# Two-layer network on one core: the compression's products on parted operands, and the mixer's low parts of weights on VectorE

## What is computed

```python
for l in range(DEPTH):                                        # DEPTH = 2
    x = x + 0.5 * rms_norm(swiglu(rms_norm(x, g1), w_in1, w_out1), p1)
    x = x + rms_norm(token_mixer(rms_norm(x, g2), ...), p2)
    x = x + 0.5 * rms_norm(swiglu(rms_norm(x, g3), w_in2, w_out2), p3)

def compress(t, pos_emb, w1, b1, w2):        # t: 256 tokens, 2 groups, 64 features
    # 15 blocks of 32 tokens, stride 16, flattened to 2048 columns for each group
    flat = blocks_of(t) + pos_emb
    return gelu(flat @ w1 + b1) @ w2         # w1: 2048 x 256

def token_mixer(h, mem, ...):
    u, bg, cg, q, kv, nsa_g, q_mem, merge_g = split(h @ w_in)
    y_conv = bg * short_conv(cg * u, conv_w)
    k_cmp, v_cmp = compress(kv[0], ...), compress(kv[1], ...)
    y_nsa = nsa_attention(q, rope(q), k_cmp, v_cmp, rope(kv[2]), kv[3], rope(kv[4]), kv[5], gates)
    y_mem = attention(q_mem, mem)
    g_conv, g_nsa, g_mem = sigmoid(merge_g)
    return (g_conv * (y_conv @ w_conv) + g_nsa * (y_nsa @ w_nsa) + g_mem * (y_mem @ w_mem)) @ w_out
```

## Time and profile before

| | |
|---|---|
| time, median of 3 runs | 1868.53 us (1867.76 to 1871.23) |
| the profiled execution: time, span | 1868.0 us, 1866.1 us |
| mean granted TensorE clock | 0.982 |
| TensorE, weight loads | 1799.1 us (96%), 1590.8 us (85%) |
| VectorE | 1107.6 us (59%), 2045 instructions |
| ScalarE | 887.0 us (48%), 1403 instructions |
| GpSimd | 205.7 us (11%), 104 instructions |
| weights | 192 chunks of 1.5 MB, 311.68 MB moved in all, 167 GB/s |

### The profile page before, as it was taken

One profiled execution on the slowest core, in us unless ns is written; L12 is line 12 of the kernel. 1 busy time (PEld: TensorE's weight loads), 2 busy tenths in 40 slices (PEclk: granted clock), 3 DMA queues, 4 the chain that ended last, 5 costly groups with the idle time before them and its releaser, 6 DMA issues.

```text
span 1866.1 us, 30310 instructions
## 1 busy us (share of the span) xinstructions
PE 1799.1 (96%) x11888; PEld 1590.8 (85%) x11888; DVE 1107.6 (59%) x2045; ACT 887.0 (48%) x1403; POOL 205.7 (11%) x104
## 2 busy tenths in 40 slices
PE   6999999999899999999999999899999999999988
PEld 5999898888789989999798988799979988767876
DVE  6555474436665556555671458455568885685764
ACT  4343353565443445343533574434455555463564
POOL 1000000655300000000002644200000000000000
PEclk9999999999999999999999999999999899799999
DMA  7454454533444544545446433445445443104421
GB/s 291 181 189 181 174 206 185 225 133 139 181 169 178 193 172 180 200 170 198 183 170 250 149 144 136 167 183 186 185 142 198 168 160 147 68 1 156 183 102 57
DMA packets 29907, 311.68 MB, mean 167 GB/s; under 512 B 3312, under 2 KB 3696, under 8 KB 4848
## 3 DMA queue, kind: packets, MB, share of 16 engines
q1 hardware_dynamic: 28944, 307.16, 44.3%
q0 software_dynamic: 864, 3.15, 0.5%
HBM read 309.24 MB, written 1.05 MB: 166 GB/s over the span
## 4 chain that ended last, share of the span: by engine, by line
PE 84%; DVE 8%; ACT 4%; issue 3%; DMA 1%; DVEq 0%; SPq 0%; ACTq 0%
PE psum L857 81%; PE psum L864 3%; DVE ring_r L489 1%; ACT region_r L483 1%; DMA ring<-in_weights 1%; ACT Sb L1773 1%; DVE Sb L2290 1%; DVE x L2193 0%; DVE region L2432 0%; DVE PTs L2401 0%; DVE region L2493 0%; DVE xs L2189 0%; ACT Sb L1667 0%; DVE region L2489 0%; DVE xs L2155 0%
## 5 line engine op out<-in xcount | busy, mean ns | idle before, releaser
L483 ACT ACTIVATE region_r<-ring 128x1024 fp32r<-128x1024 f32 x483 | 503.2, 1054 | 383.2 <-PE psum L857 355.6
L489 DVE TENSOR_TENSOR ring_r<-ring,region_r 128x1024 fp32r<-128x1024 f32 x431 | 515.2, 1221 | 166.5 <-ACT region_r L483 165.3
L857 PE MATMUL psum<-hH,region_r 128*128 128x256 f32 x2256 | 558.6, 286 | 1.4 <-DVE PTs L2401 0.9
L857 PE MATMUL psum<-xs_r,region_r 128*128 128x256 f32 x2240 | 546.8, 282 | 0.0
L857 PEld LDWEIGHTS psum<-hH,region_r 128*128 128x128 f32 x2256 | 425.5, 189 | 14.9 <-issue 8.1
L857 PEld LDWEIGHTS psum<-xs_r,region_r 128*128 128x128 f32 x2240 | 422.3, 189 | 4.8 <-issue 0.5
L857 PE MATMUL psum<-hH,ring_r 128*128 128x256 f32 x2336 | 323.0, 280 | 0.0
L857 PE MATMUL psum<-region_r 128*128 128x512 f32 x896 | 298.0, 396 | 2.7 <-DVE region_r L2231 2.1
L857 PEld LDWEIGHTS psum<-hH,ring_r 128*128 128x128 f32 x2336 | 296.2, 188 | 0.1
L857 PEld LDWEIGHTS psum<-region_r 128*128 128x128 f32 x896 | 168.2, 188 | 39.4 <-DVE region_r L2231 2.5
L857 PE MATMUL psum<-region_r,hH 128*128 128x512 f32 (+3 forms) x544 | 178.4, 363 | 15.7 <-issue 5.9
(11 more groups left out here) (236 smaller groups left out, 1946.6 us busy)
## 6 DMA issues: line engine op xcount, KB each, us to landing
ring<-in_weights SPq DMA_DIRECT2D x192, 1536.0 KB, 6.4
gpost<-in_posts POOLq DMA_DIRECT2D x6, 512.0 KB, 4.9
cst<-in_const SPq DMA_DIRECT2D x1, 1198.0 KB, 23.0
xs<-in_mem SPq DMA_DIRECT2D x1, 1024.0 KB, 5.8
x<-in_x SPq DMA_DIRECT2D x1, 1024.0 KB, 8.2
out<-x SPq DMA_DIRECT2D x2, 512.0 KB, 2.7
pars<-in_par SPq DMA_DIRECT2D x1, 368.0 KB, 6.2
p<-in_par SPq DMA_DIRECT2D x1, 206.0 KB, 22.9
```

What stands on the lines that cost most here:

```text
L483: eng.activation(unit.high, unit.raw, ACT.Copy).then_inc(h_ready, 1)
L489: eng.tensor_tensor(unit.low, unit.raw, unit.high.bitcast(F32), ALU.subtract).then_inc(l_ready, 1)
L857: ins = pe.matmul(bank, lhsT, rhs, start=start, stop=stop)
```

## The change

**Compression.** Its weights become eight units (`CMP_UNITS`, in three chunks instead of four; a second empty chunk keeps the layer's count) with high and low parts like all others; their high parts lie where the gates', one place of `gpost` and the ring's highs have room (`CMP_PLACES`). Behind the sums of kc and vc VectorE parts the block columns into `flat_parts`, high and low side by side: 60 columns instead of 30. One product with 60 stationary columns then gives high rows and low rows at once; each unit has four with its high part and four with its low part, 64 in all. The two halves of the 60 rows are summed in `hidden_turned`, now a matmul with a constant 60x30 matrix of two identities ("pair") in place of a transpose. (The low by low product is part of the sum too.)

**Low parts.** All low parts of weights in the mixer, and tile 0's `input_low` ahead of ffn2, are made by VectorE; GpSimd keeps `input_low` at the first two norms and issues the `gpost` loads, the third of which now waits until the key half of the compression's hidden tile has been read, since its place holds a high part before. ScalarE makes the high part of ffn2's third unit before `post` of tile 1 instead of behind it.

```diff
-FFN_CHUNKS, A_CHUNKS, B_CHUNKS, C_CHUNKS, D_CHUNKS = FT, 8, 1, 2, 4
-GATE_CHUNKS, BRANCH_CHUNKS, OUT_CHUNKS = 8, 4, 3
+FFN_CHUNKS, A_CHUNKS, B_CHUNKS, C_CHUNKS, D_CHUNKS = FT, 8, 1, 2, 3
+GATE_CHUNKS, EMPTY_CHUNKS, BRANCH_CHUNKS, OUT_CHUNKS = 8, 2, 4, 3
...
+CMP_UNITS = [*range(3 * AT_D, 3 * AT_D + 8)]
+CMP_PLACES = [("gate", 0), ("gate", 1), ("gate", 2), ("cmp", 0)] + [("ring", n) for n in range(4)]
...
+        cmp_highs = [gpost_r[:, 0, :]]
+        flat_parts = region_r[:, at_y + CF * SEQ:at_y + CF * SEQ + 2 * 16 * 4 * NCMP]\
+            .rearrange("p (c j h n) -> p c j h n", c=2, j=16, h=2)
...
+                    if j < 2:
+                        norm_low(1 + j + 3 * lay[0])
+                    pool.wait_ge(x_ready, 2 + 6 * lay[0] + (2 if j == 2 else 0))
                     if j == 2:
-                        low_part(pool, U_FFN2 + AHEAD_2)
-
-                    pool.wait_ge(x_ready, 2 + 6 * lay[0] + (2 if j == 2 else 0))
+                        Job("hid", 0).wait_emptied(pool)
                     pool.dma_start(gpost[:, slot, :], posts[3 * lay[0] + j].partition_broadcast(P))\
                         .then_inc(gp_full[slot], 16)
-                    if j == 1:
-
-                        pool.wait_ge(l_ready, Split(U_GATE).count - 1)
-                        lows(GATE_UNITS + BRANCH_UNITS)
-                        pool.wait_ge(l_ready, Split(U_FFN2).count - 1)
-                        lows(range(U_FFN2, U_FFN2 + AHEAD_2))
...
-                    if n == 3 * GATE_CHUNKS - 3:
-                        chunk(AT_EMPTY)
-                        used.append(w_used[AT_EMPTY % SLOTS])
+                    if n in (3 * GATE_CHUNKS - 3, 3 * GATE_CHUNKS - 2):
+                        empty = AT_EMPTY + n - (3 * GATE_CHUNKS - 3)
+                        chunk(empty)
+                        used.append(w_used[empty % SLOTS])
...
                     for m in range(2):
-                        turn(job.bank[:, m * P:(m + 1) * P], usb[:, c, m * P:(m + 1) * P], job.full if m else None)
+                        mm(job.bank[:, m * P:m * P + 2 * NCMP], usb[0:4 * NCMP, c, m * P:(m + 1) * P],
+                           C("pair")[0:4 * NCMP, :], True, True, job.full if m else None)
 
                 for c in range(2):
-                    Job("kc" if c == 0 else "vc", 0).wait_emptied(pe)
+                    pe.wait_ge(flat_ready, 2 * lay[0] + c + 1)
                     job = Job("hid", c)
                     job.wait_empty(pe)
-                    for jj in range(16):
-                        if jj % 8 == 0:
-                            w = chunk(AT_D + 2 * c + jj // 8)
-                        mm(job.bank[0:2 * NCMP, 0:256], flat[:, c, jj, :, :].rearrange("p g n -> p (g n)"),
-                           w[:, jj % 8 * 256:(jj % 8 + 1) * 256], jj == 0, jj == 15, job.full if jj == 15 else None)
-                        if jj % 8 == 7:
-                            used.append(w_used[(AT_D + 2 * c + jj // 8) % SLOTS])
+                    for n in range(4):
+                        u = CMP_UNITS[4 * c + n]
+                        unit = Split(u)
+                        for part, (ready, w) in enumerate(((h_ready, unit.high), (l_ready, unit.low))):
+                            pe.wait_ge(ready, unit.count)
+                            for j in range(4):
+                                first, last = n == part == j == 0, n == j == 3 and part
+                                mm(job.bank[0:4 * NCMP, 0:256],
+                                   flat_parts[:, c, 4 * n + j].rearrange("p h n -> p (h n)"),
+                                   w[:, j * 256:(j + 1) * 256], first, bool(last), job.full if last else None)
+                        used.append(h_room)
+                        if u % 3 == 2 or u == CMP_UNITS[-1]:
+                            used.append(w_used[u // 3 % SLOTS])
                 hidden_turned(0)
                 gate_tile(0)
...
+                    if n >= len(MIX_TILES) - 2:
+                        for u in CMP_UNITS[2 * (n - len(MIX_TILES) + 2):][:2]:
+                            high_part(act_, u)
...
+                    for u in CMP_UNITS[4:6] if i == 0 else CMP_UNITS[6:7]:
+                        high_part(act_, u)
...
+                high_part(act_, CMP_UNITS[7])
...
-                    copy(job, usb[0:2 * NCMP, c, :], job.bank[0:2 * NCMP, 0:256])
+                    copy(job, usb[0:4 * NCMP, c, :], job.bank[0:4 * NCMP, 0:256])
...
-                    post("mixed", 1.0, [i], doubled=True)
                     if i == 1:
                         split(U_FFN2, AHEAD_2, AHEAD_2 + 1)
+                    post("mixed", 1.0, [i], doubled=True)
                     norm(k + 1, tiles=[i])
...
-                if dst is None and 1 in tiles:
-                    input_low(dve, k, 1, 0)
-                    input_low(dve, k, 1, 1)
+                if dst is None:
+                    for i in tiles:
+                        if i or name == ("ffn", 1):
+                            input_low(dve, k, i, 0)
+                            input_low(dve, k, i, 1)
...
-            def attention(tag, units, evacuate, extra=None):
+            def attention(tag, units, evacuate, extra=None, gate_low=lambda n: None):
...
+                        gate_low(EARLY_GATES + 1 + 2 * s)
                         front(s)
+                        gate_low(EARLY_GATES + 2 + 2 * s)
...
+                    if n >= len(MIX_TILES) - 2:
+                        for u in CMP_UNITS[2 * (n - len(MIX_TILES) + 2):][:2]:
+                            low_part(dve, u)
...
                                         own(ins)
+                        job.wait_emptied(dve)
+                        own.settle()
+                        whole = flat[:, c].rearrange("p j g n -> p j (g n)")
+                        own(dve.tensor_copy(flat_parts[:, c, :, 0, :], whole))
+                        own.settle()
+                        dve.tensor_tensor(flat_parts[:, c, :, 1, :], whole, flat_parts[:, c, :, 0, :].bitcast(F32),
+                                          ALU.subtract).then_inc(flat_ready, 1)
                     rotated()
...
+                for u in CMP_UNITS[4:]:
+                    low_part(dve, u)
+                for u in GATE_UNITS[:3]:
+                    low_part(dve, u)
...
+                low_part(dve, GATE_UNITS[3])
                 dve.wait_ge(cmp_exp, lay[0] + 1)
...
+                low_part(dve, GATE_UNITS[4])
...
                         branch_low(Y_STEPS.index(s - 1))
...
-                attention("mix", MIX_UNITS, evacuate, lows)
+                    if s > len(MIX_UNITS):
+                        for u in BRANCH_UNITS[s - len(MIX_UNITS) - 1:][:1]:
+                            if s < len(MIX_UNITS) + 3:
+                                low_part(dve, u)
+
+                def gate_low(n):
+                    if n < N_GATE:
+                        low_part(dve, GATE_UNITS[n])
+
+                attention("mix", MIX_UNITS, evacuate, lows, gate_low)
                 for g in (4, 5):
                     branch_low(g)
+                for u in BRANCH_UNITS[2:4]:
+                    low_part(dve, u)
...
-                        if (m, b) == (6, 1):
-                            dve.wait_ge(l_ready, Split(U_OUT).count - 1)
+                        n = 3 * m + b
+                        if n % 2 == 0 and 4 <= n // 2 + 2 < N_BRANCH:
+                            low_part(dve, BRANCH_UNITS[n // 2 + 2])
...
+                split(U_FFN2, 0, AHEAD_2)
                 for i in range(NT):
+                    if i == 1:
+                        split(U_FFN2, AHEAD_2, AHEAD_2 + 1)
                     post("mixed", p, 1, lay[0] + 1, [i])
```

23 lines of the change are left out of this document (15 added, 8 removed).

## The result

The changed kernel takes 1837.32 us (median of 4 runs, 1833.57 to 1838.62) against 1868.97 us (1867.76 to 1871.23) for the kernel before beside it: a ratio of 0.9826, 95% interval 0.9813 to 0.9838. That is 31.6 us faster. The profiled execution has a span of 1836.8 us.

The account below looks back on a forecast made before the run. TensorE, busy 96% of the span, was taken as the bound. Terms −9.1 −3.4 −4.0 −2.9 −3.4 = −22.8, with +0.8 giving −22, took 1868.0 us to 1846.0; the median 0.5 above gave 1846.5, range 1840 to 1857.

Parts of the forecast that it names:

- compression and next weights: Mixer: cheaper compression products and an earlier gate chunk load save 4.2 us in layer 0, 4.9 in layer 1: 9.1.
- attention's first step: First score tile: VectorE, no longer held up by GpSimd, ends TensorE's 1.68 us wait; 1.7 us per layer, 3.4.
- branches: Mixer branches after attention: earlier start and fewer waits from locked VectorE adds, 2.0 us per layer, 4.0 together.
- step to ffn2: Chain to TensorE's restart at 512.31: VectorE's sum falls from 2.67 to 1.22 us; 2.9 us for two layers.
- clock in the mixer stages: Three stretches at 1.2 GHz after TensorE waits, worth up to 6.8 us; half taken back as waits shrink: 3.4.
- small late arrivals: A gpost load moved behind the compression products and a branch chunk waiting for gate 23's slot: a loss of 0.8 us.
- the rival of 219: Compression: a 60-column product costs 219 ns and nothing is gained; +12.8 us, about 1859 us; chance 0.04.
- The parts: VectorE's copy and subtraction of 128x480 after kc and vc: 1.2 us, bounds 0.8 and 1.5, costing TensorE 1.2 per layer.
- The rival of late transfers: Gate chunk lands after 9.0 us instead of 6.3 (+5.4), branch chunk late (+4): 1852 to 1856 us; chance 0.19.
- The rival that VectorE becomes the bound: Attention: low parts in VectorE's queue lengthen each of eight steps by 2.4 us, +38, 1884 us; chance 0.06.
- The two lows ahead of the first gated product: Branches: two VectorE low parts, 2.4 us, delay the product that frees branch 2's bank: 442.8 instead of 443.6.
- The lock: A VectorE instruction with both inputs in SBUF stands still during a GpSimd low part, some 1.6 us each.

Follow-up runs that it names:

- kernel at the old places: Changed kernel with the pair matrix in a buffer behind all others, so every other buffer lies where it lay before: 1845.27 us, ratio 0.9868.
- the kernel with the compression alone: Changed kernel with all moved low parts back on GpSimd, at the new addresses, ScalarE's earlier high part kept: 1850.05 us, ratio 0.9885.
- the kernel before shifted: Kernel before with 128 unused bytes behind the constants, so every buffer behind them lies 128 bytes higher: 1858.66 us against 1870.59, ratio 0.9937.

## Why the prediction was wrong, and where it was right

**The step that failed** is the one that isn't in the sum: the constant was listed with "the rest of the diff" and costed at nothing, and my sum took the duration of every product that isn't edited as unchanged. But those products are not unchanged: 6816 of them are in the three forms above, and the shift is worth 8 to 12 us. The kernel at the old places takes 1845.27 us where I forecast 1846.5. That this is so near is in part luck: against the 1870.59 us beside it 25.3 us are won where the sum has 22, and the terms below don't all come out.

**The terms**, measured by how far that kernel is ahead of before at the same instruction of TensorE. Its timeline behind the turn of the values' hidden tile, at attention's first step, and behind attention; in before these instructions start at 335.25, 356.85 and 442.16:

```profile
331.19 0.42 PE L865 MATMUL psum<-region,pl 128*64 128x15 f32 x8 [0.28 <-ACT region L1862]
...
350.43 0.47 PE L865 MATMUL psum<-hH,act_r 128*128 128x256 f32 x1
...
433.68 0.36 PE L865 MATMUL psum<-region_r,hH 128*128 128x256 f32 x1
```

| term | forecast, two layers | measured |
|---|---|---|
| compression and next weights | 9.1 | 8.1 (4.2 and 3.9) |
| attention's first step | 3.4 | 4.4 (2.4 and 2.1) |
| branches | 4.0 | 4.3 (1.6 and 2.7) |
| step to ffn2 | 2.9 | 2.8 (1.5 and 1.3) |
| clock in the mixer stages | 3.4 | 2.9 |
| small late arrivals | −0.8 | not seen |
| sum | 22.0 | 22.5 |

At 1199 us it is 22.5 ahead, at its end 25.8: the tail, which the change doesn't touch, had shorter stretches at half clock in this execution.

**Compression.** 64 products with 60 columns in 7.57 us, 118 ns each; I had taken 118.8, and the rival of 219 fell. The parts are 0.41 + 0.66 = 1.07 us on VectorE and 1.09 on TensorE's wait, for 1.2. The chain of waits of the changed kernel still goes through the gate chunk:

```profile
316.83 6.37 DMA ring<-in_weights
...
979.03 7.58 DMA ring<-in_weights
...
992.48 24.47 PE psum L862 x200
```

The landing took 6.37 us (I took 6.3) and 7.58 in layer 1, and TensorE resumed 5.88 and 5.87 us behind it, as before. Layer 0 gave 4.2 us, as forecast. The rival of late transfers was true in layer 1, by 1.3 us, and that is what its 3.9 lacks against 4.9.

**Attention's first step.** The wait of 1.68 us went in both layers, as forecast. I had counted the wait alone. The more is in two places: TensorE's start at that step comes 2.03 us sooner in both layers, 0.35 more than the row's idle time of 1.68, since the ends of products are modelled; and in layer 0 another 0.35 us come at 336.33, where the wait fell from 0.66 to 0.29. The rival that VectorE becomes the bound didn't come: 52 of 76.5 us, TensorE full, the low parts a step behind their highs.

**Branches.** The two lows ahead of the first gated product hold TensorE up as foreseen, by 0.88 us at 433.07. The lock was the right cause: the 32 adds took 1129 ns beside GpSimd's low parts and 426 without. The Trainium skill (SBUF — State Buffer, Who interferes with whom) says that a VectorE instruction with two inputs in SBUF contends with a GpSimd one that reads SBUF; by that page the trace agrees. The scale of 16 columns has one tensor input and fell from 1.82 to 0.18 us too, and in the kernel with the compression alone, where GpSimd has its low parts, it took 1.83. How the 4.3 us divide from the clock is not certain: layer 0, without a stretch at half clock, gave 1.6, and layer 1's 2.7 hold some of the clock's gain (see below).

**Step to ffn2.** 1.23 us for the sum in place of 2.67, all of it on the way; the wait ahead of 499.10 stayed at 1.74. The size was right. Of the two edits that stand there, ScalarE's earlier high part alone would have given it.

**Clock.** Of the three stretches, 3.4, 3.4 and 6.8 us, that behind the wait of 1.97 us at 1120.11 went, worth 1.7. The two behind the norms' waits stayed, in the kernel at the old places with 3.4 instead of 6.8. Half came out, but by luck: my reason was that the waits shrink, and the kernel before shifted, whose waits are those of before, has the same two differences. Its wait in layer 1's branches is still 1.97 us, and the clock stays at 1.00 behind it:

```profile
1111.23 0.48 PE L858 MATMUL psum<-region_r,hH 128*128 128x256 f32 x2 [1.97 <-issue]
```

```profile
1111.20:1114.60 3.40, 3.37 (x28) 3.40 (x29) 1.28 (x4) 1.06 (x1) 2.52 (x2) 1.00 0.00 0
```

There it gained 2.9 us on before between 1120 and 1150 us without any edit: beside the stretch at half clock, before waits 0.27 us at 1130.72 and 0.99 at 1133.41 for a gated product behind a locked add (2.08 and 2.32 us), and the shifted kernel has neither wait. The stretches move from one execution to the next, and what the change did to them isn't shown.

The Trainium skill (SBUF — State Buffer, Who interferes with whom) gives TensorE two independent read ports, for the moving operand and for the weights. If one took that to mean that the places of the two have no effect on each other, the runs show otherwise: 113.9 against 119.7 ns in kernels that differ by 192 unused bytes alone, and the measurement decides.

## What to carry to other kernels

A constant, a spare buffer or a longer table moves all that is allocated behind it. Where a diff changes the size of any buffer, compare the start addresses of the hot operands within 256 bytes, and cost "nothing" only where they stay; when two traces are compared, first follow the lead through stages that the change doesn't touch. In a kernel bound by TensorE, try a few spares of 64 to 192 bytes between moving operands and weights, and measure each: here one line gave 17.6 us, more than either half of the change, and another cost 21 (1858.14 us). And when VectorE rows of one shape come at two durations, look for GpSimd at the long ones. Where one half of a change is taken out, check in its trace that the other half's gains are really gone.

## What the runs showed of the hardware

- The rate of back-to-back fp32r products of 256 columns depends on where the two operands lie against each other within 256 bytes: 113.5 to 120.2 ns, a spread of 6%. A shift of both by 64 bytes changes nothing (1838.19 against 1837.32 us). The distance of the two is not all that acts.
- The products of 512 columns don't follow the same order. With ring_r moving and hH stationary their starts are 226.7 ns apart at distance 0, 227.8 to 232.1 at 64, 232.3 at 128 and 233.0 to 233.5 at 192. With ring_r moving and region_r stationary they are at 238 and 239 in the two kernels where region begins 128 bytes from ring within 256, and at 229.9 to 233.8 in all others.
- At the best distances there are two levels, 113.5 and 117.8 ns, at different times of one execution. Not explained.
- A product with 60 stationary columns takes as long as one with 128, 118 ns.
- A VectorE instruction with one input in SBUF, 16 columns wide, took 1.82 us beside a low part on GpSimd and 0.18 without it.
